# Mixer gates of a two-layer block: wide and narrow products with a bank per 128 features, halves added on VectorE, the square of the decay on ScalarE

## What is computed

```python
def rg_lru(u, w_a, b_a, w_x, b_x, lam):
    r = sigmoid(einsum('bshd,hde->bshe', uh, w_a) + b_a)
    i = sigmoid(einsum('bshd,hde->bshe', uh, w_x) + b_x)
    log_a = -LRU_C * r * softplus(-lam)
    a = exp(log_a)
    bx = sqrt(-expm1(2.0 * log_a)) * (i * u)
    _, h = associative_scan(_lru_combine, (a, bx), axis=1)
    return h

def hybrid_mixer(h, w_in, ...):
    proj = h @ w_in
    u_pool, u_lru, u_gelu, g_logits = ...
    y_pool = pool_mixer(u_pool, pool_w, pool_b, pool_scale) @ w_pool_up
    v = causal_depthwise_conv(u_lru, conv_w, conv_b)
    y_lru = (rg_lru(v, ...) * gelu(u_gelu)) @ w_lru_up
    g = sigmoid(g_logits)
    g_pool, g_lru = g[..., :D_MODEL], g[..., D_MODEL:]
    return (g_pool * y_pool + g_lru * y_lru) @ w_out
```

## Time and profile before

| | us |
|---|---|
| median of three runs | 2227.3 |
| lowest and highest | 2225.85 and 2228.28 |
| the profiled execution, in all | 2227.68 |
| its span | 2225.9 |
| TensorE busy | 1919.5 (86%) |
| VectorE busy | 1060.5 (48%) |
| ScalarE busy | 686.2 (31%) |

### The profile page before, as it was taken

How to read it: one execution, slowest core, us unless ns; L and a number is a source line. 1 busy time by engine, 2 the same in 40 slices (tenths; PEclk the granted TensorE clock), 3 DMA queues, 4 the chain that set the end, 5 groups by cost and what they waited for, 6 DMA issues and landing times.

```text
span 2225.9 us, 29282 instructions
## 1 busy us (share of the span) xinstructions
PE 1919.5 (86%) x12539; PEld 1409.2 (63%) x12539; DVE 1060.5 (48%) x1276; ACT 686.2 (31%) x777; POOL 23.5 (1%) x23
## 2 busy tenths in 40 slices
PE   8999766666666666676899999999999999999998
PEld 7775222222222222222588899998888889999888
DVE  5773000000000000000487777887778767788776
ACT  4543000000000000000344448454444444845344
POOL 0100000000000000000000001000000000100000
PEclk9999887888888878878999999999999999999999
DMA  9789999999999999999855755555575575555554
GB/s 370 251 352 423 430 429 431 430 430 429 430 431 430 431 430 430 432 431 432 336 189 154 209 177 198 168 206 189 146 230 189 154 206 180 191 170 203 190 153 135
DMA packets 226175, 658.20 MB, mean 296 GB/s; under 512 B 5476, under 2 KB 120596, under 8 KB 209428
## 3 DMA queue, kind: packets, MB, share of 16 engines
q1 hardware_dynamic: 226068, 656.67, 76.7%
HBM read 655.60 MB, written 1.05 MB: 295 GB/s over the span
## 4 chain that ended last, share of the span: by engine, by line
PE 64%; DMA 34%; SPq 1%; DVE 1%; issue 0%; ACT 0%; DVEq 0%
PE psum L1415 13%; DMA ring<-in_w_up_e_dram 11%; DMA ring<-in_w_down_e_dram 11%; DMA ring<-in_w_gate_e_dram 11%; PE psum L1556 7%; PE psum L1419 7%; PE psum L1440 5%; PE psum L1441 5%; PE psum L1442 5%; PE psum L1251 4%; PE psum L1558 4%; PE psum L1273 1%; PE psum L1576 1%; SPq L731 1%; DMA ring<-in_w_ada_dram 1%; PE psum L890 1%
## 5 line engine op out<-in xcount | busy, mean ns | idle before, releaser
L2575 DVE TENSOR_TENSOR ring_r<-ring,ring_r 128x2048 fp32r<-128x2048 f32 (+2 forms) x180 | 437.5, 2461 | 85.2 <-ACT ring_r L1918 85.0
L1918 ACT CAST ring_r<-ring 128x2048 fp32r<-128x2048 f32 (+2 forms) x180 | 360.4, 2042 | 298.4 <-PE psum L1558 114.6
L1251 PE MATMUL psum<-ring,work 128*32 128x512 f32 x1520 | 230.9, 756 | 124.0 <-DMA ring<-in_w_up_e_dram 89.8
L1415 PE MATMUL psum<-work_r,ring_r 128*128 128x512 f32 x1280 | 305.3, 391 | 0.0
L1415 PEld LDWEIGHTS psum<-work_r,ring_r 128*128 128x128 f32 x1280 | 235.2, 188 | 45.5
L1440 PE MATMUL psum<-work_r,ring_r 128*128 128x256 f32 x928 | 263.7, 284 | 0.0
L1441 PE MATMUL psum<-work_r,ring_r 128*128 128x256 f32 x928 | 262.3, 283 | 0.0
L1442 PE MATMUL psum<-work_r,ring_r 128*128 128x256 f32 x928 | 262.0, 282 | 0.0
L1251 PEld LDWEIGHTS psum<-ring,work 128*32 128x32 f32 x1520 | 54.2, 133 | 255.8 <-issue 146.0
L2543 DVE TENSOR_TENSOR work<-work,psum 128x512 f32<-128x512 f32 x16 | 11.0, 687 | 418.0 <-PE psum L1251 418.0
L1440 PEld LDWEIGHTS psum<-work_r,ring_r 128*128 128x128 f32 x928 | 177.2, 191 | 1.2 <-ACT work L2042 0.6
(11 more groups left out here) (358 smaller groups left out, 2153.8 us busy)
## 6 DMA issues: line engine op xcount, KB each, us to landing
ring<-in_w_gate_e_dram SPq DMA_DIRECT2D x23, 4096.0 KB, 33.4
ring<-in_w_down_e_dram SPq DMA_DIRECT2D x45, 2048.0 KB, 31.9
ring<-in_w_up_e_dram SPq DMA_DIRECT2D x22, 4096.0 KB, 36.7
ring<-in_ffn_w_up_dram SPq DMA_DIRECT2D x39, 2048.0 KB, 7.9
ring<-in_w_in_dram SPq DMA_DIRECT2D x25, 2048.0 KB, 8.3
ring<-in_ffn_w_down_dram SPq DMA_DIRECT2D x32, 1408.0 KB, 7.0
work<-in_w_down_e_dram SPq DMA_DIRECT2D x16, 2048.0 KB, 31.9
work<-in_w_up_e_dram SPq DMA_DIRECT2D x8, 4096.0 KB, 35.1
```

Of the source, the lines that this page charges most:

```text
L1251: mm = pe.matmul(dst[32 * g:32 * g + 32, :], xe[:, 2 * q + k, :], w[:, k, 512 * g:512 * (g + 1)], start=(q == 0 and k == 0), stop=(q == FB ...
L1415: pe.matmul(dst, w_hi[:, k, cols], h_both(k), start=(k == 0), stop=False)
L1918: act.copy(hi_unit(name, unit), raw_unit(name, unit)).then_inc(hi_ready, 1)
L2575: dve.tensor_tensor(lo_unit(name, unit), raw_unit(name, unit), hi_unit(name, unit).bitcast(F32), ALU.subtract).then_inc(lo_ready, 1)
```

## The change

The gate groups are made with `paired_passes` and get two banks each. In the list of banks the gap of unused ones before the `dn` groups is now taken once and not in halves. VectorE takes a gate out with a reduce over the two halves, waits for its own result, and multiplies with `rstd_row` in place; the sigmoid on ScalarE waits for that (`gate_scaled_ready`). ScalarE makes `decay_sq` with Square, behind the tanh and ahead of the gelus, and VectorE's multiply for it is gone.

```diff
--- before.py
+++ after.py
@@ -182,7 +182,7 @@
     mixer += [(("g", g), "dve") for g in range(8)]
     mixer += [(("pup", g), "dve") for g in range(4)] + [(("lup", g), "dve") for g in range(8)]
     mixer += [(("out", g), "dve") for g in range(4)]
-    return ffn(0) + [(name, e, 1) for name, e in mixer] + ffn(1)
+    return ffn(0) + [(name, e, 2 if name[0] == "g" else 1) for name, e in mixer] + ffn(1)
 
 
 class Groups:
@@ -198,7 +198,7 @@
         self.first, at = [], 0
         for name, _, w in groups:
             if name[0] == "dn" and name[2] == 0:
-                at += -sum(self.width) % BANKS // 2
+                at += -sum(self.width) % BANKS if name[1] == 0 else 0
             assert at % w == 0
             self.first.append(at % BANKS)
             at += w
@@ -554,6 +554,7 @@
         l_sq, l_sum, l_ms, l_std = sem("l_sq"), sem("l_sum"), sem("l_ms"), sem("l_std")
         l_x = sem("l_x")
         h_hi_ready, h_lo_ready = sem("h_hi_ready"), sem("h_lo_ready")
+        gate_scaled_ready = sem("gate_scaled_ready")
         silu_done, v_base, gelu_done, gate_done = sem("silu_done"), sem("v_base"), sem("gelu_done"), sem("gate_done")
         ident_r_ready = sem("ident_r_ready")
         u_hi_ready, u_lo_ready = sem("u_hi_ready"), sem("u_lo_ready")
@@ -1603,7 +1604,7 @@
                     project(("gelu", 3 + q), ("proj", 5), q)
                 for i in range(4):
                     for q in range(2):
-                        project(("g", 2 * i + q), ("proj", 6 + i), q)
+                        paired_passes(("g", 2 * i + q), ("proj", 6 + i), q)
                 pe.wait_ge(pool_mix_lo_ready, l + 1)
                 for q in range(4):
                     three_passes(("pup", q), ("pup", 0), q // 2, pool_mix_hi, pool_mix_lo, 2, first=2 * (q % 2))
@@ -2021,7 +2022,7 @@
                     act.activation(part, part, ACT.Gelu_apprx_tanh).then_inc(gelu_done, 1)
 
                 def gate(g):
-                    wait_emptied(("g", g))
+                    act.wait_ge(gate_scaled_ready, l * 8 + (g + 1))
                     part = gs_[:, 512 * g:512 * (g + 1)]
                     act.activation(part, part, ACT.Sigmoid).then_inc(gate_done, 1)
 
@@ -2063,6 +2064,8 @@
                     ins = act.activation(rgate[:, c, :], rgate[:, c, :], ACT.Tanh,
                                          scale=lc[:, n_layer + HEADS + c:n_layer + HEADS + c + 1])
                 ins.then_inc(decay_ready, 1)
+                act.wait_ge(group_done, groups.done(("pmix", 1), l))
+                act.activation(decay_sq, decay_, ACT.Square).then_inc(decay_ready, 1)
                 for g in range(5):
                     gelu(g)
                 split(("proj", 7), l)
@@ -2111,7 +2114,7 @@
 
             act.wait_ge(l_ms, 3 * LAYERS + 1)
             act.activation(std[:, 0:TT], bank[6][:, 0:TT], ACT.Sqrt, bias=EPS).then_inc(l_std, 1)
-            act.wait_ge(dve_layer, LAYERS * 56 + 1)
+            act.wait_ge(dve_layer, LAYERS * 55 + 1)
             act.wait_ge(outT_done, 2 * TT)
             for t in range(TT):
                 act.mul(out_tok[:, t, 0:512], bank[2 * t], rstd_col[:, t:t + 1]).then_inc(out_ready_act, 1)
@@ -2632,7 +2635,7 @@
                     dve.sem_inc(lo_ready, 2)
 
             for l in range(LAYERS):
-                step = Steps(dve, dve_layer, 56, l)
+                step = Steps(dve, dve_layer, 55, l)
 
                 def done(name):
                     dve.wait_ge(group_done, groups.done(name, l))
@@ -2765,7 +2768,14 @@
                     scaled_flat(gel_[:, 512 * g:512 * (g + 1)], ("gelu", g))
 
                 def gate_scaled(g):
-                    scaled_flat(gs_[:, 512 * g:512 * (g + 1)], ("g", g))
+                    done(("g", g))
+                    first = 512 * groups.bank(("g", g))
+                    part = gs_[:, 512 * g:512 * (g + 1)].rearrange("p (c t) -> p c t", c=2)
+                    dve.tensor_reduce(part, psum[:, first:first + 1024].rearrange("p (c b t) -> p c t b", c=2, b=2), AX.X,
+                                      ALU.add).then_inc(emptied["dve"], 1)
+                    wait_emptied(("g", g))
+                    dve.tensor_tensor(part, part, rstd_row[:].unsqueeze(1).broadcast_to([P, 2, S]),
+                                      ALU.mult).then_inc(gate_scaled_ready, 1)
 
                 step(dve.memset(upad[:, :, 0:TAPS - 1], 0.0))
                 split(("proj", 2), l)
@@ -2813,11 +2823,10 @@
                 dve.wait_ge(v_ready, l * 5 + 5)
                 step(dve.tensor_tensor(i_, i_, v_, ALU.mult))
 
-                dve.wait_ge(decay_ready, l + 1)
-                step(dve.tensor_tensor(decay_sq, decay_, decay_, ALU.mult))
                 split(("proj", 7), l)
                 gate_scaled(0)
                 gate_scaled(1)
+                dve.wait_ge(decay_ready, 2 * l + 2)
                 dve.scalar_tensor_tensor(out=r_, in0=decay_sq, scalar=1.0, in1=r_, op0=ALU.add,
                                          op1=ALU.mult).then_inc(m2_ready, 1)
 
@@ -2898,7 +2907,7 @@
 
             dve.wait_ge(l_std, 3 * LAYERS + 1)
             dve.reciprocal(rstd_col[:, 0:TT], std[:, 0:TT]).then_inc(dve_layer, 1)
-            dve.wait_ge(dve_layer, LAYERS * 56 + 1)
+            dve.wait_ge(dve_layer, LAYERS * 55 + 1)
             dve.wait_ge(outT_done, 2 * TT)
             for t in range(TT):
                 dve.tensor_scalar(out_tok[:, t, 512:1024], bank[2 * t + 1], rstd_col[:, t:t + 1], None,
```

## The result

The changed kernel takes 2232.8 us (median of 11 runs, 2229.93 to 2234.42), the kernel before 2227.46 us (2225.85 to 2228.28) beside it. The ratio is 1.0022, with a 95% interval of 1.0014 to 1.0030: slower by about 5 us. That it is slower is clear; on which side of the 0.2% that the prediction takes as its threshold it lies is not, since the interval reaches from 0.14 to 0.30%. The forecast was 2231.3 us, "no difference" with 0.62 and slower with 0.35, range 2226.5 to 2234.5.

What follows compares the result with a forecast made beforehand. TensorE was taken to set the time, with VectorE having 6.6 us to spare beside the gates. Later lup starts (+2.5 us) and one clock fall (+1.5) add 4.0 us to 2227.3, giving 2231.3 us, range 2226.5 to 2234.5.

Steps and rivals of the forecast that it cites:

- The gain of the wide form: TensorE's gate groups in the mixer: 5.567 us instead of 5.76, saving 0.193 us a group, 3.1 us for both layers.
- 1.25 us more for a gate on VectorE: VectorE's reduce, wait and multiply per gate take 1.86 us instead of 0.61, 10.0 us more a layer.
- Square on ScalarE, cost nothing: Before the gates, moving the 2.82 us multiply off VectorE to ScalarE, priced there at 2.35 us, costs the path nothing.
- Banks cost nothing: Gate groups holding two of six banks wait for older reduces; nearest case gate 5, six microseconds of margin, no cost.
- The scan on time, nothing paid behind it: VectorE starts the scan at 1400.46 against 1400.37 us; gates 6 and 7 behind it delay gel_lo to 1423.66.
- +2.5 us from the waits: TensorE waits some 2.5 us before lup, which starts 1.23 us later a layer; +2.5 us for two layers.
- The clock: TensorE's clock falls to 1.2 GHz behind about one in two of the waits before lup; one fall likeliest, +1.5 us.
- the forecast's one fall: TensorE's clock falls behind one of the two waits before lup, +1.5 us, giving 2231.3 us; chance 0.39.
- the first rival: The waits before lup come but TensorE's clock falls behind neither: 2229.8 us, chance 0.22.
- the second rival: TensorE's clock falls behind the waits in both layers: 2232.8 us, or 2233 to 2235 if longer; chance 0.26.
- VectorE isn't late: Rival: lru_ready comes by 1421.0 us before lup, so TensorE keeps its 3.1 us: 2224.2 us, chance 0.10.
- The wide form gains nothing here: Rival: a gate group in the mixer still takes 5.76 us, VectorE's chain comes later: 2233.6 us, chance 0.03.

Runs made afterwards that it cites:

- six-wide: Changed kernel with gates 6 and 7 narrow again with one multiply, and the bank gap in two halves: 2223.96 us, ratio 0.9985.
- gates-alone: Changed kernel with the square of the decay put back as a multiply on VectorE: 2233.25 us, ratio 1.0028.
- late-products: Changed kernel with VectorE's multiplies of gates 6 and 7 moved behind its last subtraction for lup: 2225.96 us, ratio 0.9996.
- one-more: Changed kernel with one more 128x2560 multiply on VectorE right before the last subtraction: 2239.43 us, ratio 1.0054.
- e3_warm: Changed kernel with 20 unused 256-column matmuls before TensorE's wait for the first lup group: 2230.16 us, ratio 1.0013.
- look2: Changed kernel run again unaltered for one profile: 2229.43 us.
- look3: Changed kernel run again unaltered for another single profile: 2230.79 us.

## Why the prediction was right, point by point

- **The gain of the wide form**, 0.193 us a group: exact (5.567 us). The estimate by a fixed cost of 2.5 ns a matmul (the Trainium skill, TensorE: Matmul & The Clock Gate, Back-to-back issue gap, which gives it for matmuls by themselves) was 0.04; the groups of the profile after and the shorter mixers of the six-wide kernel speak against it for this shape.
- **1.25 us more for a gate on VectorE**: the starts of reduce and next operation at gate 5 are 1397.06 and 1398.93, 1.87 apart for 0.61 before; 1.26.
- **Square on ScalarE, cost nothing**: right (1.0002), and that its place in VectorE's chain is what keeps gate 5 on time is shown by the gates-alone kernel.
- **Banks cost nothing**: right for the changed kernel. That a gap of four banks would have cost 1.6 us a layer I had not worked out, and met it in my own experiments.
- **The scan on time, nothing paid behind it**: right to 0.02 us at the scan and 0.04 at the end of the last subtraction; the six-wide, late-products and one-more kernels each move the wait by what they put in or take out.
- **+2.5 us from the waits**: 2 x 1.25, as measured in the two profiles without a fall, with the 20 matmuls (e3_warm) and without them (look2). The 0.07 us that TensorE was to take to start behind VectorE stood on no row; the profile shows 0.05 (1422.15 to 1422.20).
- **The clock**: price 1.5, measured 1.5 to 1.6. One fall in two was the rate; 5 of 8 were seen, over the four profiles of the changed kernel 2, 2, 0 and 1. So the forecast's one fall turned up once (2230.79 us, look3), the first rival's none once (2229.43 for 2229.8), the second rival's two twice (2231.93 and 2232.69 for 2232.8). The median is 5.3 us above the kernel before, where one fall gives 4.1 and two give 5.6, and it equals the second rival's number. If a step was too small, it is the number of falls; but the interval of the difference, 3.1 to 6.7 us, holds both counts, and the expert stage's spread of 3.7 us is in it. So that 2231.3 was 1.5 us from the median says little about the count: the wait and the price of a fall are confirmed, the count stays open.
- **VectorE isn't late** fell: VectorE has no idle time from the start of gate 5 to the last subtraction but 0.03 to 0.04 us behind each reduce and 0.20 us before the split at 1416.59, which waits for the cast. **The wide form gains nothing here** fell with the 5.567 us.

## What to carry to other kernels

Work that is moved off a full engine has to be laid against the stretch in which the other engine is full, not against its mean: VectorE had 6.6 us to spare beside the gates, but none between scan and `lup`, and two of eight gates stood there. Convert what lies ahead of that stretch and leave what lies in it: the six-wide version keeps three quarters of the gain and wins, with 0.27 us of margin before `lup`. And a wait of a few microseconds on TensorE is to be priced with a fall of its clock behind it, here once in about two times (6 of 12 waits of 2.5 to 2.65 us).

## What the runs showed of the hardware

- A wait of 2.53 us on TensorE between dense work at 2.4 GHz went with 3.4 us at 1.2 GHz in five of eight cases, one of 2.64 us in one of four, a wait of 5.27 us with 6.8 us in two of two; waits of 0.8 us (six) and 1.3 us (four) with none. One fall costs 1.5 to 1.6 us of work with 256 columns (starts 0.21 to 0.22 us apart for 0.12).
- Twenty unused products of 256 columns in a wait that is there anyway cost nothing: mixers of 191.97 us, as the changed kernel has them without a fall. That they hold the clock is likely from the medians (2230.16 for 2232.80 us) and not shown by the one profile.
- The expert stage, the same in all kernels here, ends up to 3.7 us apart from profile to profile. Differences of a few microseconds between two profiles have to be read from stage lengths, which repeat within 0.2 us.
